# Depthwise convolution on TensorE: four 32-row matmuls side by side in place of one 128-row matmul

## The reference

```python
def conformer_conv_module(h, w_pw1, b_pw1, w_dw, b_dw, ln_g, ln_b, w_pw2, b_pw2):
    d = h.shape[-1]
    a = jnp.einsum("bsd,de->bse", h, w_pw1) + b_pw1
    u = a[..., :d] * jax.nn.sigmoid(a[..., d:])
    u = causal_dwconv(u, w_dw, b_dw)          # 31 taps for each channel
    u = jax.nn.silu(layernorm(u, ln_g, ln_b))
    return jnp.einsum("bsd,de->bse", u, w_pw2) + b_pw2
```

## Time and profile before

| | before |
|---|---|
| median of three runs | 950.11 us |
| the profiled execution's own time | 950.07 us |
| its span | 948.3 us |
| granted TensorE clock, mean | 1.00 |
| TensorE busy | 938.4 us, 99% of the span |
| TensorE weight loads busy | 791.2 us, 83% |
| VectorE, ScalarE, GpSimd busy | 58%, 41%, 12% |

### The profile page before, as it was taken

How to read it: one execution, slowest core, us unless ns; L and a number is a source line. 1 busy time by engine, 2 the same in 40 slices (tenths; PEclk the granted TensorE clock), 3 DMA queues, 4 the chain that set the end, 5 groups by cost and what they waited for, 6 DMA issues and landing times.

```text
span 948.3 us, 11921 instructions
## 1 busy us (share of the span) xinstructions
PE 938.4 (99%) x4512; PEld 791.2 (83%) x4512; DVE 552.4 (58%) x703; ACT 393.4 (41%) x606; POOL 112.2 (12%) x74
## 2 busy tenths in 40 slices
PE   8999999999999999999999999999999999999997
PEld 6889899888888888888888898888888888888887
DVE  6899995657555555555434359765555655532333
ACT  7785596434333333332222355433333333322231
POOL 0558896000000000000000020000000000000000
PEclk9999999999999999999999999999999999999999
DMA  7320022233222222312232341233222232223212
GB/s 254 116 89 1 1 90 89 90 99 110 102 88 88 88 88 97 123 63 91 76 107 91 117 147 55 89 108 113 88 88 88 88 94 100 64 90 122 91 62 90
DMA packets 17020, 88.56 MB, mean 93 GB/s; under 512 B 2016, under 2 KB 4320, under 8 KB 9952
## 3 DMA queue, kind: packets, MB, share of 16 engines
q1 hardware_dynamic: 16416, 87.67, 27.2%
q10 hardware_dynamic: 576, 0.52, 0.2%
HBM read 86.09 MB, written 2.10 MB: 93 GB/s over the span
## 4 chain that ended last, share of the span: by engine, by line
PE 97%; DMA 1%; SPq 1%; DVE 0%; ACT 0%; issue 0%; DVEq 0%
PE bank L1138 29%; PE bank L1139 29%; PE bank L1140 29%; PE bank L1190 2%; PE bank L1191 2%; PE bank L1189 2%; DMA w_raw<-w_pw 1%; PE bank L1480 1%; PE bank L1224 1%; PE bank L1207 0%; PE bank L1448 0%; PE bank L1453 0%; PE bank L1452 0%; PE bank L1213 0%; PE bank L1342 0%; SPq L302 0%
## 5 line engine op out<-in xcount | busy, mean ns | idle before, releaser
L1138 PE MATMUL bank<-h_hi,w_hi 128*128 128x512 f32 x800 | 312.4, 390 | 1.4 <-DVE w_lo L768 1.4
L1140 PE MATMUL bank<-h_hi,w_lo 128*128 128x512 f32 x800 | 311.3, 389 | 0.0
L1139 PE MATMUL bank<-h_lo,w_hi 128*128 128x512 f32 x800 | 311.2, 389 | 0.0
L455 ACT ACTIVATE w_hi<-w_raw 128x2048 fp32r<-128x2048 f32 (+2 forms) x87 | 147.3, 1693 | 214.3 <-PE bank L1140 214.3
L768 DVE TENSOR_TENSOR w_lo<-w_raw,w_hi 128x2048 fp32r<-128x2048 f32 (+2 forms) x81 | 162.2, 2002 | 100.7 <-ACT w_hi L455 100.0
L1138 PEld LDWEIGHTS bank<-h_hi,w_hi 128*128 128x128 f32 x800 | 150.2, 188 | 33.5 <-DVE w_lo L768 1.8
L1139 PEld LDWEIGHTS bank<-h_lo,w_hi 128*128 128x128 f32 x800 | 150.2, 188 | 31.7 <-issue 0.5
L1140 PEld LDWEIGHTS bank<-h_hi,w_lo 128*128 128x128 f32 x800 | 150.2, 188 | 30.8
L1139 PE MATMUL bank<-u_lo,w_hi 128*128 128x512 f32 (+1 forms) x406 | 153.3, 378 | 0.0
L1138 PE MATMUL bank<-u_hi,w_hi 128*128 128x512 f32 (+1 forms) x374 | 141.0, 377 | 0.0
L1140 PE MATMUL bank<-u_hi,w_lo 128*128 128x512 f32 (+1 forms) x374 | 140.8, 377 | 0.0
(11 more groups left out here) (212 smaller groups left out, 1001.3 us busy)
## 6 DMA issues: line engine op xcount, KB each, us to landing
w_raw<-w_up SPq DMA_DIRECT2D x44, 1024.0 KB, 4.8
w_raw<-w_down SPq DMA_DIRECT2D x32, 704.0 KB, 4.0
...
```

Source lines behind the costliest of these rows:

```text
L455: nc.scalar.activation(w_hi[s][:, 0:columns], w_raw[s][:, 0:columns], ACT.Copy).then_inc(w_rounded[s], 1)
L1138: M.matmul(dst, a, hi, start=start, stop=False)
L1139: M.matmul(dst, a, lo, start=False, stop=False)
L1140: return M.matmul(dst, b, hi, start=False, stop=stop)
```

## The change

TensorE's half of the convolution is cut otherwise. A tile's 128 channels are four quads of 32 rows. For each quad the output tokens are taken in four phases (token mod 4): 32 channels by four phases are the 128 output columns, and 128 moving columns are 512 tokens. The weights of one matmul are 32 rows by 128 columns, the taps at four neighbouring offsets. 34 offsets cover 31 taps in four phases. So `conv_tile` issues 34 x 3 sets of four matmuls, the four of a set on different rows of the array and into different banks. No tap of tile 6 goes to DVE any more. `conv_done` is counted by tile.

Around it: the blocks are built once, for all four tiles (32 ACT instructions of 592 columns, four of POOL); `round_even` and `split_even` are one instruction a tile; `cross_even` is gone; draining a tile takes 16 ACT instructions of 32x128, for tile 7 too. Slot 0 now holds the gate unit and slot 1 the value unit, so the gates come first. conv tile 0 stands before the gate unit of step 3, tile 1 before its value unit, tiles 2 and 3 after `sum_near`. The weights of pw2 no longer wait for the convolution. The near mean is taken off tiles 4 and 5 in their accumulators (`centre_sums`), off tile 7 by DVE before its last tap. The norm's sums no longer pass through DVE: ten `sum_wide` where there were five, in banks 2 and 3.

```diff
-CONV_UNITS = 2 * len(CONV_TILES)
-SHIFTS = (TAPS + 1) // 2
+QUADS = 4
+QUAD = P // QUADS
+PHASES = QUADS
+OFFSETS = TAPS + PHASES - 1
+ENTRIES = OFFSETS + PHASES - 1
+SPAN = (PAD + T + 2) // PHASES
+TP = T // PHASES
...
+SUM_STEPS = 2 * TAPS + 1
...
-BANKS_PW1 = [(0, 2), (6, 0), (2, 6), (2, 6)]
-BANKS_CONV = (0, 0, 1, 1, 0, 0, 1, 0)
+BANKS_PW1 = [(0, 2), (6, 0), (2, 6), (6, 6)]
+BANKS_CONV = ((0, 1, 2, 3), (0, 1, 2, 3), (0, 1, 2, 3), (6, 7, 0, 1))
...
+        even_hi = place("even_hi", [P, len(CONV_TILES), PHASES, SPAN], f32r, o + 13056)
+        even_lo = place("even_lo", [P, len(CONV_TILES), PHASES, SPAN], f32r, o + 13056 + 8704)
...
+                for s in range(2):
+                    sp.wait_ge(w_split[s], M_PW1 + i)
+                    sp.dma_start(w_raw[s][:, :], w_pw1[2 * i + 1 - s]).then_inc(raw_loaded[s], 16)
...
+                pool.wait_ge(even_rounded, n + 1)
+                nc.gpsimd.tensor_tensor(even_lo[:, n, :, :], by_phase(glu_even[:, n % 2, :]), as_f32(even_hi[:, n, :, :]), SUB).then_inc(even_split, 1)
+            def build_lo(n):
+                nc.gpsimd.tensor_tensor(block_lo[:, n * ENTRIES:(n + 1) * ENTRIES, :], quad_mask[:, :].unsqueeze(1).broadcast_to([P, ENTRIES, QUAD]),
+                                        as_f32(tap_lo[:, n, :]).unsqueeze(2).broadcast_to([P, ENTRIES, QUAD]), MUL).then_inc(lo_built, 1)
...
+            def build_hi(first, last):
+                for c in range(first, last):
+                    block = nc.scalar.activation(block_hi[:, :, c], flat(tap_pad[:, :, :]), ACT.Copy, scale=quad_mask[:, c:c + 1])
+                if last == QUAD:
+                    block.then_inc(hi_built, 1)
...
+                nc.scalar.activation(even_hi[:, n, :, :], by_phase(glu_even[:, n % 2, :]), ACT.Copy).then_inc(even_rounded, 1)
...
             def drain_conv(n):
-                for g in range(2):
-                    for p in range(2):
-                        bias = (col("b_dw", c) if p == g else bias_other[:, n:n + 1])[half_rows(p), :]
-                        nc.scalar.activation(conv_out[half_rows(g), c, p:T:2], bank[BANKS_CONV[2 * n + g]][half_rows(p), g * HT:(g + 1) * HT], ACT.Identity, bias=bias).then_inc(even_drained, 1)
+                act.wait_ge(conv_done, n + 1)
+                for q in (range(QUADS) if n < 3 else (2, 3, 0, 1)):
+                    for p in range(PHASES):
+                        nc.scalar.activation(conv_out[quad(q), CONV_TILES[n], PHASES - 1 - p:T:PHASES], bank[BANKS_CONV[n][q]][quad(p), 0:TP], ACT.Identity, bias=bias_out[quad(p), q, n:n + 1]).then_inc(even_drained, 1)
...
+            act.wait_ge(bias_set, QUADS * PHASES)
             drain_conv(0)
-            act.wait_ge(unit_done[0], M_PW1 + PW1_STEPS)
-            build_hi(5)
+            round_unit(0, M_PW2, UNIT)
...
+            drain_gate(0)
             scale_val(0)
-            drain_gate(0)
             multiply(0)
-            taps(0, 0, 8)
+            taps(0, 0, 4)
+            drain_gate(1)
+            taps(0, 4, 8)
             scale_val(1)
-            taps(0, 8, 13)
-            drain_gate(1)
-            taps(0, 13, 15)
             multiply(1)
-            taps(0, 15, 20)
+            taps(0, 8, 14)
+            drain_gate(2)
+            taps(0, 14, 21)
             scale_val(2)
-            taps(0, 20, 24)
-            drain_gate(2)
-            taps(0, 24, 26)
             multiply(2)
-            taps(0, 26)
-            taps(1, 0, 8)
+            taps(0, 21)
+            taps(1, 0, 2)
+            drain_gate(3)
+            taps(1, 2, 14)
             scale_val(3)
-            taps(1, 8, 15)
-            drain_gate(3)
-            taps(1, 15, 16)
             multiply(3)
-            def shared_tap(k):
...
-            taps(1, 16, 24)
-            for k in range(2 * SHARED_SHIFTS):
-                shared_tap(k)
-                taps(1, 24 + k, 25 + k)
-            taps(1, 24 + 2 * SHARED_SHIFTS)
-            mean, rest, squares = bank[BANK_MEAN][:, :], bank[BANK_REST][:, :], bank[BANK_SQUARES][:, :]
-            dve.wait_ge(near_copied, 1)
-            dve.wait_ge(drained[1], DRAINED_PW1 + PW1_STEPS)
-            for t in range(2):
-                dve.wait_ge(tap_step[t], 2 * TAPS)
-                V.scalar_tensor_tensor(conv_out[:, 4 + t, :], mean, -1.0, conv_out[:, 4 + t, :], MUL, ADD).then_inc(dev_late, 1)
-            dve.wait_ge(even_drained, 12)
-            dve.wait_ge(shared_step, 2 * SHARED_SHIFTS)
-            V.tensor_tensor(conv_out[:, SHARED_TILE, :], bank[BANK_SHARED][:, :], conv_out[:, SHARED_TILE, :], ADD).then_inc(dev_late, 1)
-            dve.wait_ge(dev_early, 4)
-            for n, c in enumerate((5, 6, 3)):
...
-            def drain_last(g):
-                c, n = CONV_TILES[-1], len(CONV_TILES) - 1
-                dve.wait_ge(conv_done, 2 * n + g + 1)
-                dve.wait_ge(near_copied, 1)
-                for p in range(2):
-                    bias = (col("b_dw", c) if p == g else bias_other[:, n:n + 1])[half_rows(p), :]
-                    V.scalar_tensor_tensor(conv_out[half_rows(g), c, p:T:2], bank[BANKS_CONV[2 * n + g]][half_rows(p), g * HT:(g + 1) * HT], bias, near_mean[half_rows(p), p:T:2], ADD, SUB).then_inc(dev_last, 1)
-            drain_last(0)
-            for n, c in enumerate((5, 6)):
-                dve.wait_ge(dev_squared, c + 1)
-                if n:
-                    dve.wait_ge(squares_late, n)
-                V.tensor_tensor(squares if n == 0 else dev_sq[:, 4, :], squares, dev_sq[:, c, :], ADD).then_inc(squares_late, 1)
-            drain_last(1)
+            taps(1, 14, CENTRED_AT)
+            centre_sums()
+            taps(1, CENTRED_AT, TAPS - 1)
+            dve.wait_ge(even_drained, 4 * QUADS * PHASES)
+            V.tensor_tensor(conv_out[:, 7, :], conv_out[:, 7, :], near_mean, SUB).then_inc(dev_last, 1)
+            taps(1, TAPS - 1)
...
-            def conv_unit(u, between=None):
-                n, g = u // 2, u % 2
...
-                dst = bank[BANKS_CONV[u]][:, g * HT:(g + 1) * HT]
-                first = SHARED_SHIFTS if CONV_TILES[n] == SHARED_TILE else 0
-                for k in range(first, SHIFTS):
-                    hi, lo = (x[:, 3 * n + 2 * g, k:k + HT] for x in (even_hi, even_lo))
-                    a, b = conv_hi[u][:, k * P:(k + 1) * P], conv_lo[u][:, k * P:(k + 1) * P]
-                    M.matmul(dst, a, hi, start=k == first, stop=False, skip_group_check=True)
-                    M.matmul(dst, a, lo, start=False, stop=False, skip_group_check=True)
-                    last = M.matmul(dst, b, hi, start=False, stop=k == SHIFTS - 1, skip_group_check=True)
-                    if between:
-                        between(k)
+            def conv_tile(n):
+                pe.wait_ge(hi_built, 1)
+                pe.wait_ge(lo_built, n + 1)
+                pe.wait_ge(even_rounded, n + 1)
+                pe.wait_ge(even_split, n + 1)
+                for m in range(OFFSETS):
+                    at_block = slice(n * ENTRIES + m, n * ENTRIES + m + PHASES)
+                    for w, x, first, final in ((block_hi, even_hi, m == 0, False), (block_hi, even_lo, False, False), (block_lo, even_hi, False, m == OFFSETS - 1)):
+                        for q in range(QUADS):
+                            last = M.matmul(bank[BANKS_CONV[n][q]][:, 0:TP], flat(w[quad(q), at_block, :]), x[quad(q), n, m % PHASES, m // PHASES:m // PHASES + TP], start=first, stop=final, skip_group_check=True)
                 last.then_inc(conv_done, 1)
...
+            pw1_unit(0, 1)
+            for i in (1, 2):
+                for s in range(2):
+                    pw1_unit(i, s)
+            wait_drained((2, 3), DRAINED_PW1 + 3)
+            for t in range(2):
+                pe.wait_ge(glu_done[t], 2)
+            conv_tile(0)
+            pw1_unit(3, 0)
+            pe.wait_ge(even_drained, QUADS * PHASES)
+            conv_tile(1)
+            pw1_unit(3, 1)
             sum_near()
-            conv_unit(3)
-            conv_unit(4)
-            conv_unit(5)
-            conv_unit(6)
-            conv_unit(7, sum_rest)
-            pe.wait_ge(squares_late, 2)
-            sum_wide(dev_sq[:, 4, :], start=False, stop=False, at_bank=BANK_SQ_TOK)
-            keep_busy(2, BANK_REST)
-            pe.wait_ge(dev_last, 4)
-            sum_wide(conv_out[:, 7, :], start=False, stop=True).then_inc(dev_summed, 1)
-            pe.wait_ge(dev_squared, KD + 1)
-            sum_wide(dev_sq[:, 7, :], start=False, stop=True, at_bank=BANK_SQ_TOK).then_inc(squares_summed, 1)
+            pe.wait_ge(near_copied, 1)
+            conv_tile(2)
+            for t in range(2):
+                pe.wait_ge(glu_done[t], PW1_STEPS)
+            pe.wait_ge(even_drained, 2 * QUADS * PHASES + 2 * PHASES)
+            conv_tile(3)
+            pe.wait_ge(even_drained, 3 * QUADS * PHASES)
+            pe.wait_ge(dev_early, 4)
+            sum_wide(conv_out[:, 3, :], start=True, stop=False, at_bank=BANK_DEV)
```

(22 more changed lines are left out.)

304 lines of the change are left out of this document (103 added, 201 removed).

## The result

**The changed kernel takes 994.58 us (median of 4 runs, 993.63 to 997.04) against 950.09 us in the same session: a ratio of 1.0474, with a 95% interval of 1.0461 to 1.0487.** Forecast were 967.0 us and a range of 946 to 990: the sign came out, the size did not, and the time lies outside the range. The profiled execution took 994.43 us with a span of 992.6.

The account below looks back on a forecast made before the run. PE, busy 99%, was taken to bound the kernel until pw2 starts. That start moves from 151.67 to 122.9 + 4C, so four tiles' 45.7 us less 28.8 add 16.9 to 950.11: 967.0 us, range 946 to 990.

Parts of the forecast that it names:

- 0. s at full clock, C: Convolution on PE: s, a set of four matmuls, takes 0.112 us; C, a tile of 102 sets, 11.4 us.
- 1, 2. tile 2 starts at 102.8 + 2C: Step 3's value unit ends at 98.2 + 2C; scalings, multiply, rounding, POOL and hand-over add 4.6 us before tile 2.
- 3, 4. tiles 2 and 3, 2C: The last two convolution tiles on PE take C each, so tile 3 ends at 105.8 + 4C.
- 3. eight drains ahead of tile 3: Tile 3 waits for tile 2's first eight drains: 2.6 us at 0.33 each, and 0.4 to hand over.
- 4. sixteen drains: After tile 3, sixteen drains take 5.3 us and 0.3 more, ending at 111.4 + 4C.
- 4. `keep_busy`: Behind the last drains, eight `keep_busy`, 16 records of 0.115, take 1.8 us and hide DVE's subtraction.
- 5. six sums: Behind `keep_busy`, six norm sums of 0.9 us on PE take 5.5 us, where two stood before.
- 6. last sum to pw2: From the last sum's end to the pw2 product's start: unchanged at 4.16 us.
- rival E: PE's clock falls in the idle gaps ahead of tiles 2 and 3: 1.5 to 3 us more; no separate chance.
- the likeliest case: Weight loads set a set's time, 0.105 to 0.13 us: 967.0 us, own range 963 to 975, chance 0.37.
- Rivals A, B and C: Time of a set: A 0.065 to 0.071 us, chance 0.32; B 0.071 to 0.105, 0.12; C 0.13 to 0.2, 0.11.
- D: A set's four matmuls run one after another: 0.444 us a set, +152 us, 1102 us; chance 0.08.

Follow-up runs that it names:

- the filled kernel: Changed kernel with dummy 128-row matmuls filling TensorE's three idle stretches, ahead of tile 2, ahead of tile 3 and ahead of the last drain's end: 972.57 us, ratio 1.0232.

## Why the prediction was wrong in size

Its sum, taken apart against the trace of the kernel after:

| step of the prediction | forecast | measured | difference of the start of pw2 |
|---|---|---|---|
| 0. s at full clock, C | 0.112; 11.4 | 0.111; 11.54 | in the next row |
| 1, 2. tile 2 starts at 102.8 + 2C | 125.6 | 126.14 | +0.5 |
| 3, 4. tiles 2 and 3, 2C | 22.8 | 22.03 + 22.05 | +21.3 |
| 3. eight drains ahead of tile 3 | 3.0 | 4.25 | +1.3 |
| 4. sixteen drains | 5.6 | 8.1 | +2.5 |
| 4. `keep_busy` | 1.8 | 3.4 | +1.6 |
| 5. six sums | 5.5 | 5.5 | 0 |
| 6. last sum to pw2 | 4.16 | 4.16 | 0 |

They add up to 27.2 us, and pw2 started 27.1 us behind the forecast 168.6.

**The step that failed** is the price of rival E: "If tile 2 ran so for 3 to 6 us, it would cost 1.5 to 3 us more in every case." The sum that gave 967.0 held nothing for the clock at all, and the range only these 3 us or so. The two gaps stood where they were foreseen (4.17 us for about 4, 4.25 for 3), and the idea that the clock falls in them was right. What was assumed without a row is that the clock would come back after 3 to 6 us behind these sets as it does behind full-width matmuls. The kernel before with the same gap bears that price out for full-width matmuls, at its lower end, 1.4 us. Behind sets of 32 rows by 128 columns it did not come back in 22 us, and the filled kernel gives the size of the mistake: 22.0 us. Without the clock's part the change takes 972.6 us, inside the likeliest case's own range of 963 to 975, near its upper end because of the drains.

**The second step**, the drains, was mis-sized. "In proportion to the elements 0.33" was interpolated from 0.24 for 64 elements and 0.50 for 256. The 64-element row was a copy between SBUF tiles and not a drain of a bank; the nearer row was the other drain, and 0.50 us is what these drains of 128 elements cost. It is 24 drains by 0.17, 4 us, and stood in the range as its upper end. It is no fixed price of an instruction on a bank either. In the same trace ACT brings 512 neighbouring columns of a bank out in 0.60 us (122.01) and four columns in 0.17. The drains of the change write every fourth token, those of before every second; no run here tells whether that is the reason.

**Two small terms.** Both were misjudged with little effect on the time. The block builds are 32 instructions of 128x148 in the trace and not of 592 columns, as the description of the change and the prediction have it, and eight pass in 2.77 us, 0.35 each, so that all take some 11 us and not 22.4. Rounding one tile's moving operand takes 1.1 us and not 0.7 (two in 2.25 at 123.14); it lies on the path, in the hand-over ahead of tile 2, and its 0.4 us went under in other small differences there.

**What was right.** The weight load sets the pace: 0.111 us a set in tiles 0 and 1, half of it with half the weight columns, the same at full clock with half the moving columns, four times as much on shared rows. Rivals A, B and C are out by the first, D by the last. The path (tile 2 behind POOL's `even_lo`, tile 3 behind the drains, DVE idle at the end, for 36.6 us in place of some 10 since PE came so late) is the trace's, and the six sums and the last step are right to 0.1 us.

The Trainium skill's rule on weight loads (TensorE: Matmul & The Clock Gate, LDWEIGHTS), that 32 rows take as long as 128 and the columns count, agrees with the trace: on 32 rows 0.111 us for 128 columns, as the one-column matmuls on 128 rows, and 0.058 for 64. The Trainium skill's 3.07 for four row pieces of 512 moving columns (the same page, Measured speedup vs the span model) does not carry over to these of 128. Here four on the same rows against four on their own give 0.445/0.111, 4.0 times, the most that the Trainium skill promises for 32 rows (TensorEngine Tiling (Array Packing), Theoretical Speedup). It brought nothing all the same, since the matmul that it replaced paid one load for 256 moving columns, 0.119 us.

PE was busy for 21.86 of 22 us with sets, and the granted clock stayed at 0.50. The Trainium skill (TensorE: Matmul & The Clock Gate, What's actually happening) says that the clock is set "based on how busy the PE has been recently". By the rows the busy time alone does not decide it, and here the measurement counts.
